# FFN layers of an S5 and retention trunk: double buffers for the sums of u, another order of the plain units, one difference on GpSimd

## What is computed

```python
def rmsnorm(x, g):
    xf = x.astype(jnp.float32)
    y = xf * lax.rsqrt(jnp.mean(jnp.square(xf), axis=-1, keepdims=True) + NORM_EPS)
    return (y * g.astype(jnp.float32)).astype(x.dtype)

def swiglu(u, w_gate, w_up, w_down):
    h = jax.nn.silu(u @ w_gate.astype(u.dtype)) * (u @ w_up.astype(u.dtype))
    return h @ w_down.astype(u.dtype)

# in each layer, behind its mixer:
x = x + swiglu(rmsnorm(x, ffn_norm[i]), ffn_w_gate[i], ffn_w_up[i], ffn_w_down[i])
```

## Times and profile before

| | |
|---|---|
| runs | 1277.39, 1278.86, 1279.42 us |
| median | 1278.86 us |
| the profiled execution's own time | 1278.51 us |
| its span | 1276.7 us |
| PE busy | 1225.5 us (96%) |
| DVE busy | 856.2 us (67%) |
| ACT busy | 533.0 us (42%) |
| POOL busy | 64.0 us (5%) |
| mean granted clock of PE | 0.99 |

### The profile page before, as it was taken

How to read it: one execution, slowest core, us unless ns; L and a number is a source line. 1 busy time by engine, 2 the same in 40 slices (tenths; PEclk the granted TensorE clock), 3 DMA queues, 4 the chain that set the end, 5 groups by cost and what they waited for, 6 DMA issues and landing times.

```text
span 1276.7 us, 18841 instructions
## 1 busy us (share of the span) xinstructions
PE 1225.5 (96%) x7693; PEld 1076.3 (84%) x7693; DVE 856.2 (67%) x1009; ACT 533.0 (42%) x693; POOL 64.0 (5%) x84
## 2 busy tenths in 40 slices
PE   3989997999999999999999999999997999999997
PEld 3778887889988998888888888888877889989986
DVE  8897768568856868746555564634467578857864
ACT  5655545325533545333342234322355335523532
POOL 5940000000000000000000000000000000000000
PEclk9999998999999999999999999999998999999998
DMA  5563332333342333313323132233323333333321
GB/s 115 150 126 100 99 91 75 101 98 100 100 131 67 101 102 112 119 54 108 99 66 107 34 129 76 66 99 99 99 66 99 100 100 100 100 101 98 91 75 66
DMA packets 166521, 121.89 MB, mean 95 GB/s; under 512 B 6104, under 2 KB 158736, under 8 KB 166416
## 3 DMA queue, kind: packets, MB, share of 16 engines
q1 hardware_dynamic: 164784, 118.24, 30.6%
q10 hardware_dynamic: 1664, 2.62, 1.0%
HBM read 114.29 MB, written 2.10 MB: 91 GB/s over the span
## 4 chain that ended last, share of the span: by engine, by line
PE 90%; DVE 4%; ACT 2%; ACTq 1%; issue 1%; DMA 1%; SPq 0%; DVEq 0%
PE bank L821 16%; PE bank L822 16%; PE bank L823 16%; PE bank L876 9%; PE bank L877 9%; PE bank L878 9%; PE bank L1005 2%; PE bank L1003 2%; PE bank L1004 2%; ACTq L519 1%; DMA s<-in_x_dram 1%; PE bank L717 1%; PE bank L1031 1%; PE bank L1032 1%; PE bank L1033 1%
## 5 line engine op out<-in xcount | busy, mean ns | idle before, releaser
L1096 ACT ACTIVATE w_hi<-w_raw 128x2048 fp32r<-128x2048 f32 (+1 forms) x70 | 130.4, 1863 | 172.8 <-PE bank L823 154.0
L821 PE MATMUL bank<-u_hi,w_hi 128*128 128x512 f32 x480 | 188.5, 393 | 0.0
L822 PE MATMUL bank<-u_lo,w_hi 128*128 128x512 f32 x480 | 186.8, 389 | 0.0
L823 PE MATMUL bank<-u_hi,w_lo 128*128 128x512 f32 x480 | 186.8, 389 | 0.0
L1510 DVE TENSOR_TENSOR w_lo<-w_raw,w_hi 128x2048 fp32r<-128x2048 f32 x46 | 105.4, 2290 | 60.7 <-ACT w_hi L1096 60.5
L1500 DVE TENSOR_TENSOR tmp<-bank,tmp 128x512 f32<-128x512 f32 (+2 forms) x118 | 77.8, 659 | 88.2 <-PE bank L823 53.1
L876 PE MATMUL bank<-s_hi,w_hi 128*128 128x256 f32 x408 | 116.0, 284 | 0.0
L877 PE MATMUL bank<-s_lo,w_hi 128*128 128x256 f32 x408 | 115.9, 284 | 0.0
L878 PE MATMUL bank<-s_hi,w_lo 128*128 128x256 f32 x408 | 115.8, 284 | 0.0
L821 PE MATMUL bank<-hid_hi,w_hi 128*128 128x512 f32 x288 | 113.0, 392 | 0.9 <-issue 0.9
L822 PE MATMUL bank<-hid_lo,w_hi 128*128 128x512 f32 x288 | 112.2, 389 | 0.0
(11 more groups left out here) (274 smaller groups left out, 2725.3 us busy)
## 6 DMA issues: line engine op xcount, KB each, us to landing
w_raw<-in_ret_w_qkvg_dram SPq DMA_DIRECT2D x24, 1024.0 KB, 5.0
w_raw<-in_ffn_w_up_dram SPq DMA_DIRECT2D x44, 512.0 KB, 3.7
w_raw<-in_ffn_w_gate_dram SPq DMA_DIRECT2D x44, 512.0 KB, 4.8
w_raw<-in_ffn_w_down_dram SPq DMA_DIRECT2D x16, 1024.0 KB, 5.0
w_raw<-in_ret_w_o_dram SPq DMA_DIRECT2D x8, 1024.0 KB, 5.2
w_raw<-in_ffn_w_down_dram SPq DMA_DIRECT2D x8, 768.0 KB, 4.4
w_raw<-in_s_glu_w_dram SPq DMA_DIRECT2D x4, 1024.0 KB, 5.2
s<-in_x_dram ACTq DMA_DIRECT2D x8, 256.0 KB, 8.1
```

The lines of the kernel that those rows point to most:

```text
L821: pe.matmul(o, w_hi[w][:, w_cols], hi, start=first, stop=False)
L822: pe.matmul(o, w_hi[w][:, w_cols], lo, start=False, stop=False)
L823: return pe.matmul(o, w_lo[w][:, w_cols], hi, start=False, stop=end)
L1096: return act.activation(o, i, ACT.Copy, scale=scale)
```

## The change

`s_raw`, `a_raw` and `b_raw` get a second buffer, indexed by k % 2; `u_sums(k)` and `scaled_u(k)` wait for k-2 instead of k-1. `s_raw` now overlays `r_hi0` and a part of `r_lo0`, so `raw_high` of the first S unit of set 0 waits for all splits of u. The difference of the token halves of `a_raw` (part 3 of `s_raw`) is made by POOL in `u_difference`, which signals `diff_ready`; `u_sums_high` and `scaled_u` wait for it too. DVE makes three sums instead of four. `FACTORS_AT` and `prepare` go, and the orders of ACT and DVE in the blocks n = 1 to 4 are written out anew:

```diff
-        s_raw = sb(lap, "s_raw", [P, 4, HALF])
+        s_raw = sb(lap, "s_raw", [P, 2, 4, HALF])
...
-        a_raw = sb(over, "a_raw", [P, SEQ])
+        a_raw = sb(over, "a_raw", [P, 2, SEQ])
...
 # ACT
             def scaled_u(layer, k, gain_col):
-                if k:
-                    act.wait_ge(s_raw_ready, KH * layer + k)
+                if k > 1:
+                    act.wait_ge(s_raw_ready, KH * layer + k - 1)
+                    act.wait_ge(diff_ready, KH * layer + k - 1)
...
             def u_sums_high(layer, k):
                 act.wait_ge(s_raw_ready, KH * layer + k + 1)
+                act.wait_ge(diff_ready, KH * layer + k + 1)
...
             def raw_high(layer, n):
...
+                if unit.z == 0 and s == 0:
+                    act.wait_ge(s_split, KH * (layer + 1))
...
                     if unit.kind == "C":
                         if n == 0:
                             continue
+                        if kind(n + 1) == "C":
+                            plain_high(layer, n + 1)
+                        else:
+                            raw_high(layer, n + 1)
                         if n == 1:
                             root(norm)
-                            high(n + 1)
+                            scaled_u(layer, 0, gain_col)
+                            scaled_u(layer, 1, gain_col)
                             silu(n - 1)
-                            hidden_high(n - 1)
                             continue
+                        if n == 2:
+                            u_sums_high(layer, 0)
+                            hidden_high(n - 2)
                         silu(n - 1)
...
+                        if n < KH:
+                            scaled_u(layer, n, gain_col)
+                        else:
+                            sum_high(layer, n + 1, 0)
+                            sum_high(layer, n + 1, 1)
+                        u_sums_high(layer, n - 1)
                         hidden_high(n - 1)
...
 # DVE
             def u_sums(layer, k):
+                raw, a, b = s_raw[:, k % 2, :, :], a_raw[:, k % 2, :], b_raw[:, k % 2, :]
                 dve.wait_ge(a_ready, KH * layer + k + 1)
-                if k:
-                    dve.wait_ge(s_split, KH * layer + k)
-                dve.tensor_tensor(s_raw[:, 3, :], a_raw[:, 0:HALF], a_raw[:, HALF:SEQ], ALU.subtract)
+                if k > 1:
+                    dve.wait_ge(s_split, KH * layer + k - 1)
...
                         if n == 1:
+                            split_weights(0, pair + 1)
                             inverse_rms(norm)
                             clear_sum()
+                            gate_out(n - 1)
+                            u_sums(layer, 0)
+                            continue
                         gate_out(n - 1)
-                        up_out(n - 1)
...
+                        if n == 2:
+                            hidden(n - 2)
+                        elif n == 3:
+                            hidden_low(n - 2)
+                        if kind(n + 1) == "C":
+                            split_weights((n + 1) % 2, PAIR0[f"ffn{layer}"] + (n + 1) // 2)
+                            u_sums(layer, n - 1)
+                            if n == 2:
+                                u_sums_low(layer, 0)
+                                hidden_low(n - 2)
+                                hidden(n - 1)
+                                continue
                             hidden(n - 1)
+                            u_sums_low(layer, n - 2)
                             hidden_low(n - 1)
+                            sums(layer, n + 2, 0)
+                            sums(layer, n + 2, 1)
                             continue
...
+                        u_sums(layer, n - 1)
+                        raw_low(layer, n + 1)
                         hidden(n - 1)
...
+                        u_sums_low(layer, n - 2)
+                        sum_low(layer, n + 1)
+                        u_sums_low(layer, n - 1)
                         hidden_low(n - 1)
...
 # POOL
+            def u_difference(layer, k):
+
+                a = a_raw[:, k % 2, :]
+                pool.wait_ge(a_ready, KH * layer + k + 1)
+                if k > 1:
+                    pool.wait_ge(s_split, KH * layer + k - 1)
+                pool.tensor_tensor(s_raw[:, k % 2, 3, :], a[:, 0:HALF], a[:, HALF:SEQ],
+                                   ALU.subtract).then_inc(diff_ready, 1)
+
+            for layer in range(2):
+                for k in range(KH):
+                    u_difference(layer, k)
```

More of the change, by code:

```diff
@@ L1266, in u_sums_high @@
                 act.wait_ge(s_raw_ready, KH * layer + k + 1)
-                copy(s_hi[:, k, :, :], s_raw[:, :, :]).then_inc(s_hi_ready, 1)
+                act.wait_ge(diff_ready, KH * layer + k + 1)
+                copy(s_hi[:, k, :, :], s_raw[:, k % 2, :, :]).then_inc(s_hi_ready, 1)
             def raw_high(layer, n):
@@ L1794, in u_sums @@
             def u_sums(layer, k):
+                raw, a, b = s_raw[:, k % 2, :, :], a_raw[:, k % 2, :], b_raw[:, k % 2, :]
                 dve.wait_ge(a_ready, KH * layer + k + 1)
-                if k:
-                    dve.wait_ge(s_split, KH * layer + k)
-                dve.tensor_tensor(s_raw[:, 3, :], a_raw[:, 0:HALF], a_raw[:, HALF:SEQ], ALU.subtract)
-                step(dve.tensor_tensor(s_raw[:, 0, :], a_raw[:, HALF:SEQ], b_raw[:, HALF:SEQ], ALU.add))
+                if k > 1:
+                    dve.wait_ge(s_split, KH * layer + k - 1)
+                step(dve.tensor_tensor(raw[:, 0, :], a[:, HALF:SEQ], b[:, HALF:SEQ], ALU.add))
                 settle()
-                step(dve.tensor_tensor(s_raw[:, 1, :], s_raw[:, 0, :], a_raw[:, 0:HALF], ALU.subtract))
+                step(dve.tensor_tensor(raw[:, 1, :], raw[:, 0, :], a[:, 0:HALF], ALU.subtract))
                 settle()
-                dve.tensor_tensor(s_raw[:, 2, :], b_raw[:, 0:HALF], s_raw[:, 1, :], ALU.subtract).then_inc(s_raw_ready, 1)
+                dve.tensor_tensor(raw[:, 2, :], b[:, 0:HALF], raw[:, 1, :], ALU.subtract).then_inc(s_raw_ready, 1)
             def u_sums_low(layer, k):
                 dve.wait_ge(s_hi_ready, KH * layer + k + 1)
-                dve.tensor_tensor(s_lo[:, k, :, :], s_raw[:, :, :], s_hi[:, k, :, :].bitcast(F32),
+                dve.tensor_tensor(s_lo[:, k, :, :], s_raw[:, k % 2, :, :], s_hi[:, k, :, :].bitcast(F32),
                                   ALU.subtract).then_inc(s_split, 1)
@@ L1830, in raw_low @@
                 unit, s = UNITS[n], n % 2
-                dve.wait_ge(s_split, KH * (layer + 1))
+                if unit.z == 0 and s == 0:
+                    dve.wait_ge(s_split, KH * (layer + 1))
                 dve.wait_ge(r_hi_ready[s], SEVENS[s] * layer + unit.z + 1)
@@ L1910, in next_norm @@
                             add_square(norm + 1, t)
[L1912 to L1921, removed]
                 for n, unit in enumerate(UNITS):
@@ L1952, in chunked_hidden @@
-                        prepare(n + 1)
+                        u_sums(layer, n - 1)
+                        raw_low(layer, n + 1)
+                        hidden(n - 1)
+                        u_sums_low(layer, n - 2)
+                        sum_low(layer, n + 1)
+                        u_sums_low(layer, n - 1)
                         hidden_low(n - 1)
-                        for k in ks[1:]:
-                            u_sums_low(layer, k - 1)
-                            u_sums(layer, k)
```

42 lines of the change are left out of this document (7 added, 35 removed).

## The result

The changed kernel took 1261.79 us (median of four runs, 1260.15 to 1265.51) against 1278.34 us of the kernel before: ratio 0.9874, 95% interval 0.9851 to 0.9898. The forecast was 1262.8 in a range of 1259 to 1267. A ratio with its interval is estimated from all runs, so it can differ a little from the quotient of two medians. One execution of the old-order variant (2463.79 us) and one of the sums-late variant (1526.77 us) ran in a far slower state and are left out of their medians and ratios.

The account below looks back on a forecast made before the run. TensorE, busy 96% of the span, was the bound. Gains 9.39 + 9.52 + 0.60 = 19.51 less new gaps 3.44 gave net 16.07 us: 1278.51 to 1262.4, as median 1262.8; range 1259 to 1267.

Parts of the forecast that it names:

- The loss at unit 5: Unit 5's start: TensorE's wait for w_lo and the half-clock matmuls behind it, 9.39 and 9.52 us to gain.
- 0.30 for unit 4: Unit 4's late w_lo makes a small second gap, 0.30 us a layer, which goes.
- The new wait: Ahead of unit 2, bank 1 waits for hidden(0) behind gate_out(1): 1.54 us, with restart 1.72 us a layer.
- the restart: TensorE's slow resumption behind the new gap ahead of unit 2, 0.18 us a layer.
- the clock stays up: No clock fall in the gap ahead of unit 2; rival: half-speed matmuls, 1.74 us twice, 1266.3 us, chance 0.08.
- The walk: New order dated step by step in layer 0: w_lo of unit 5 at 197.2, unit 5 at 200.2, 3.0 us spare.
- the root at 156.8: First block, n=1: ScalarE does w_hi of unit 2 until 156.2, then the square root until 156.8.
- GpSimd's difference of k=3: Before unit 5: 0.73 us on GpSimd, at worst holding a vector operation 0.73 us, leaving 2.3 of 3.0 us spare.
- the ping-pong over one buffer: Cause given for unit 5's late w_lo: one s_raw buffer makes each k go sums, s_hi, s_lo before the next sums.
- My two groups: Follow-up theory: behind unit 5's 19th matmul in layer 1, either 308.6 to 309.0 us or 305.1 to 307.0.
- at most 1.7 us from it: Clock fall behind a longer gap ahead of unit 2: rival in a follow-up forecast, up to 1.7 us a layer.

Follow-up runs that it names:

- after: The changed kernel against the kernel before; median 1261.79 us, its profiled execution 1265.51 us.
- e0: The changed kernel once more, unaltered, on another chip: 1260.06 us, ratio 0.9853 to the kernel before.
- e2: Changed kernel with the difference of the token halves back on the vector engine, GpSimd idle in the FFN layers: 1261.05 us, ratio 0.9862 to the kernel before.
- e3: Kernel before with only hidden(0) and hidden_low(0) moved behind gate_out(1): 1281.81 us against 1277.46, ratio 1.0035.
- e5: Changed kernel with each difference made eight times over on GpSimd: 1263.63 us, ratio 0.9888 to the kernel before.
- e8: Changed kernel with the sums for unit 5's weights moved back from block n=3 to n=4: 1260.57 us against 1277.46 of the kernel before, ratio 0.9862.
- e6: Changed kernel's new order with one buffer of s_raw, a_raw and b_raw: 1265.04 us, ratio 0.9895 to the kernel before.
- e9: Changed kernel with one buffer, difference on DVE, hidden(0) in block n=1, silu(0) ahead of scaled_u(1), other scaled copies at block ends: 1256.14 us, ratio 0.9829.
- e1_again: Changed kernel with hidden(0) moved back into block n=1, run once more on another chip: 1256.50 us, ratio 0.9833 to the kernel before.
- e1_hidden_early: Changed kernel with hidden(0) moved back into block n=1, behind the sums of u for k=0: 1256.23 us, ratio 0.9828 to the kernel before.

## Why the prediction was right, point by point

- **The loss at unit 5.** 9.39 and 9.52 us, with gap and half clock in one term, and 0.30 for unit 4. In the kernel with hidden(0) early the stretches are 46.57 and 46.56, 9.69 and 9.80 shorter than before: the forecast's terms were 9.69 and 9.82.
- **The new wait.** Place, cause and size held: 1.54 us predicted from unit 2's due time, 1.63 measured; the restart was 0.12 instead of 0.18, so that the whole came to 1.75 and 1.77 us for 1.72. That the clock stays up held in each of the twelve gaps of 1.5 us in the six profiles that have them unaltered (after, e0, e2, e3, e5, e8).
- **The walk.** w_lo of unit 5 was forecast 3.0 us ahead of its use, and is 3.06 ahead. Two errors in it cancelled or were covered. I had the root at 156.8; the sqrt table load of 1.28 us, which used to lie in ScalarE's idle time ahead of the rms matmul, now comes behind w_hi of unit 2 (159.16 in the trace of after), since it is issued with the root. It was hidden by w_lo of unit 2 on the vector engine, which the reciprocal waits for anyway. And GpSimd's difference of k=3 holds the t_raw operation for 0.54 us, of the 0.73 that I allowed; it took 1.06 us itself instead of 0.74.
- **The description of the cause was too wide.** The prediction called the ping-pong over one buffer the reason for the late w_lo. The old order with two buffers keeps the full wait of 15.0 us; the new order with one buffer has none worth the name (e6), and with three more steps moved none at all (e9). What was late was late by its place in the queues, with k=1 and 2 beside unit 3, k=3 beside unit 4, and the weights' splits behind all of them. Which of the moved steps is enough stays open: only the weights' sums were put back by themselves (e8), and that cost nothing. The sum didn't depend on this, so the number came out.
- **The scatter of a single profile.** The total for the profiled execution was forecast as 1262.4 and was 1265.5, 3.1 us over, although the stretches fit: 2.86 us lie ahead of the first rms matmul, in work that the change does not touch. The medians agree with the forecast, but a part of that is luck. They gained 16.6 us on the first chip and 18.7 beside e0, where the stretches gained 16.0; the remainder lies outside the stretches. It is no larger than the scatter described next, but no profile shows where it lies.

The open question of that scatter is partly answered. The part behind the 19th matmul of unit 5 in layer 1 took 308.6 to 309.0 us in nine of the fourteen profiles, before and after among them, 306.7 to 306.9 in three (e6, e8, e1_again), and 305.1 and 305.4 in e1_hidden_early and e5. PE ahead of the end in e0_after_again and then in e1_hidden_early:

```profile
1244.45 1.86 PE L1072 MATMUL bank<-ones,tmp 128*128 128x1 f32 x8 [2.63 <-DVE tmp L1768]
1246.18 3.65 PE L1066 MATMUL bank<-ident,final 128*128 128x128 f32 x16
```
```profile
1242.58 1.05 PE L1072 MATMUL bank<-ones,tmp 128*128 128x1 f32 x8 [2.63 <-DVE tmp L1768]
1243.49 1.95 PE L1066 MATMUL bank<-ident,final 128*128 128x128 f32 x16
```

The same wait of 2.63 us, and behind it 3.65 us or 1.95 for the same sixteen transposes: the clock falls or it doesn't. From the 19th matmul to this wait's end all fourteen profiles took 293.2 to 293.4 us, and from there to the end of the span 11.8 to 15.7. That is the spread of up to 3.9 us, in the kernel before as in the others, and the 3.8 us between e1_hidden_early and e0 as medians holds some of it; the 3.5 us of the stretches do not. My two groups were too coarse: e1_again's 306.9 us lies inside the second as I had drawn it (305.1 to 307.0), but the trace shows a case of its own, in which the clock fell for a part of the way.

The 2.86 us at the start of the run of after lie in the S5 mixer. PE waits there for a DMA, and the granted clock is 0.50 behind it:

```profile
84.73 1.12 PE L789 MATMUL bank<-s,s_u 128*64 128x128 f32 x8 [2.68 <-DMA s<-w_raw]
...
84.00:86.00 2.00, 1.27 (x12) 1.30 (x14) 1.93 (x3) 1.17 (x2) 0.00 (x0) 0.50 0.48 116
```

In e0 the same matmuls start at 81.76 without a wait, and the clock stays at 1.00 from 80 to 100 us. Why the DMA came late in this one execution isn't shown.

## What to carry to other kernels

When engines work through queues in program order, date every step by what it truly needs and by what waits behind it: hidden(0) could have run and stood behind a wait that was not its own, and held the bank that TensorE needed next. Price a gap by the distance between matmul starts across it and its slow wake, not by its length. Before adding buffers or another engine for a late step, try its place in the queue: here the place was all of the time gained, and buffers and GpSimd added spare time alone.

## What the runs showed of the hardware

- In the FFN none of the twelve gaps of 1.5 us lowered the granted clock, all eight of 5.1 to 7.5 us did, and gaps of 2.6 to 2.7 us did in some cases and not in others of the same length (2.56 in layer 0 yes, 2.55 in layer 1 no; 2.73 no and 2.73 yes). I had taken the fall to follow from the length alone, and I had expected at most 1.7 us from it: behind the 2.73 us gap it cost 2.84. In the S5 mixer, where TensorE is often idle, length decides even less: behind a gap of 1.82 us the clock was 0.50 (e6, the first two rows), behind one of 2.38 at the same place it was 1.00 (e2, the last two). So the twelve gaps are what this FFN shows, and no safe length for another stage.

```profile
79.67 1.66 PE L717 MATMUL bank<-s_tc,s_fb 64*16 64x128 f32 x16 [1.82 <-POOL s_tc L2254]
80.00:82.00 2.00, 2.00 (x24) 1.49 (x21) 1.93 (x4) 0.00 (x0) 0.00 (x0) 0.50 1.03 350
...
79.94 1.27 PE L717 MATMUL bank<-s_tc,s_fb 64*16 64x128 f32 x20 [2.38 <-POOL s_tc L2256]
80.00:82.00 2.00, 2.00 (x48) 1.66 (x48) 1.93 (x3) 0.03 (x1) 0.00 (x0) 1.00 1.03 326
```

- A GpSimd operation of 0.74 us and a vector operation with two SBUF inputs lengthen each other, by up to 0.54 us on the vector engine and up to 1.39 on GpSimd (2.13 under r_lo); the multiplies that read PSUM kept their 0.68 beside it.
